# Modulation steps of the second norm, regrouped between the stages of MLA's chain

## The reference

```python
def adaln(cond, w, b):
    return jnp.split(jax.nn.silu(cond) @ w + b, 6, axis=-1)   # sh1, sc1, g1, sh2, sc2, g2

def latent_layer(x, mod, cache, rows, cols, p):
    sh1, sc1, g1, sh2, sc2, g2 = mod
    h = rms_norm(x, p['norm1']) * (1 + sc1) + sh1
    (na_q, na_k, na_v), pool_in, mla_q, ckv, kpe, (sq, sk, sv) = project_mixers(h, p)
    ...
    x = x + g1 * (mixed @ p['w_out'])
    return channel_mlp(x, sh2, sc2, g2, p)

mla_q = rms_norm(heads(rms_norm(mla_cq, p['mla_q_a_norm']) @ p['mla_w_uq'], MLA_HEADS), p['mla_q_norm'])
ckv = rms_norm(mla_ckv, p['mla_kv_norm'])
```

## Time and profile before

| | |
|---|---|
| median of 3 runs | 1676.9 us (1673.57 to 1682.08) |
| the profiled execution | 1677.47 us, span 1675.5 us |
| PE busy | 1557.6 us (93% of the span) |
| PE weight loads busy | 1443.7 us (86%) |
| DVE busy | 1119.9 us (67%) |
| ACT busy | 843.8 us (50%) |
| POOL busy | 135.5 us (8%) |
| mean granted clock of TensorE | 0.972 |

### The profile page before, as it was taken

How to read it: one execution, slowest core, us unless ns; L and a number is a source line. 1 busy time by engine, 2 the same in 40 slices (tenths; PEclk the granted TensorE clock), 3 DMA queues, 4 the chain that set the end, 5 groups by cost and what they waited for, 6 DMA issues and landing times.

```text
span 1675.5 us, 29600 instructions
## 1 busy us (share of the span) xinstructions
PE 1557.6 (93%) x11426; PEld 1443.7 (86%) x11426; DVE 1119.9 (67%) x1937; ACT 843.8 (50%) x1477; POOL 135.5 (8%) x99
## 2 busy tenths in 40 slices
PE   6878997899999999999987889978999999999998
PEld 4755895589999999999976569846999999999998
DVE  4554346858788787787565434487677878878763
ACT  3555533767555454454355454357665545445442
POOL 0003003520000000000000130054000000000000
PEclk8999998999999999999999899979999999999999
DMA  9630453302222223222734205441212222322221
GB/s 323 197 115 1 75 148 111 112 26 76 76 76 76 77 76 101 65 88 76 242 111 158 72 1 130 114 151 52 76 51 76 76 77 76 101 72 81 76 76 64
DMA packets 150867, 160.23 MB, mean 96 GB/s; under 512 B 16390, under 2 KB 132808, under 8 KB 150728
## 3 DMA queue, kind: packets, MB, share of 16 engines
q1 hardware_dynamic: 150024, 158.13, 30.7%
q10 hardware_dynamic: 576, 0.16, 0.0%
q0 software_dynamic: 128, 0.05, 0.0%
HBM read 153.41 MB, written 4.65 MB: 94 GB/s over the span
## 4 chain that ended last, share of the span: by engine, by line
PE 76%; DVE 10%; ACT 9%; issue 3%; DMA 2%; ACTq 0%; SPq 0%; DVEq 0%
PE ps L1909 33%; PE ps L2282 20%; PE ps L2046 10%; PE ps L2298 3%; PE ps L1944 2%; PE ps L1888 1%; PE ps L2070 1%; ACT w_hi L905 1%; PE ps L2123 1%; DVE extrema L1561 1%; ACT pt_c L905 1%; PE ps L2101 1%; DVE extrema L1544 1%; PE ps L2018 1%; PE ps L1918 1%
## 5 line engine op out<-in xcount | busy, mean ns | idle before, releaser
L905 ACT ACTIVATE w_hi<-w_raw 128x512 fp32r<-128x512 f32 (+1 forms) x242 | 189.1, 781 | 196.4 <-PE ps L1909 91.1
L2282 PE MATMUL ps<-x_hi,w_hi 128*128 128x322 f32 x784 | 244.3, 312 | 0.6 <-DVE us L1736 0.6
L2282 PE MATMUL ps<-x_hi,w_lo 128*128 128x322 f32 x784 | 243.5, 311 | 0.0
L2282 PE MATMUL ps<-x_lo,w_hi 128*128 128x322 f32 x784 | 243.4, 310 | 0.0
L1909 PE MATMUL ps<-z_hi,w_hi 128*128 128x384 f32 (+1 forms) x1024 | 233.7, 309 | 0.0
L1909 PE MATMUL ps<-z_hi,w_lo 128*128 128x384 f32 (+1 forms) x1024 | 233.1, 309 | 0.0
L1909 PE MATMUL ps<-z_lo,w_hi 128*128 128x384 f32 (+1 forms) x1024 | 233.1, 309 | 0.0
L1331 DVE TENSOR_TENSOR w_lo<-w_raw,w_hi 128x512 fp32r<-128x512 f32 x212 | 146.8, 692 | 36.0 <-ACT w_hi L905 27.7
L1909 PEld LDWEIGHTS ps<-z_hi,w_hi 128*128 128x128 f32 x1024 | 157.2, 188 | 0.0
L1909 PEld LDWEIGHTS ps<-z_lo,w_hi 128*128 128x128 f32 x1024 | 156.2, 188 | 0.0
L1909 PEld LDWEIGHTS ps<-z_hi,w_lo 128*128 128x128 f32 x1024 | 156.2, 188 | 0.0
(11 more groups left out here) (299 smaller groups left out, 2968.4 us busy)
## 6 DMA issues: line engine op xcount, KB each, us to landing
w_raw<-in_mlp_w SPq DMA_DIRECT2D x64, 1024.0 KB, 5.3
ada_own<-in_w_ada SPq DMA_DIRECT2D x54, 512.0 KB, 4.5
w_raw<-in_w_in SPq DMA_DIRECT2D x14, 1024.0 KB, 9.0
ada_mix<-in_w_ada SPq DMA_DIRECT2D x21, 512.0 KB, 7.3
ada_room<-in_w_ada SPq DMA_DIRECT2D x15, 512.0 KB, 9.1
w_raw<-in_w_out SPq DMA_DIRECT2D x8, 768.0 KB, 5.2
ada_first<-in_w_ada SPq DMA_DIRECT2D x6, 512.0 KB, 9.0
x_in<-in_x_sample SPq DMA_DIRECT2D x1, 2048.0 KB, 8.6
```

What stands on the lines that cost most here:

```text
L905: do(nc.scalar.activation(out, in_, ACT.Copy), sem)
L2282: last = M.matmul(bank(b, XW), w[r][:, k, :], x_of(x, x_name)[:, k, :], start=k == 0 and q == 0 and not more, stop=k == 3 and q == 2, skip ...
```

## The change

```diff
@@ -619,7 +619,7 @@
         def late_ticks(l, stage):
-            cuts = (0, 0, 4, 9, 14, 18)
+            cuts = (0, 0, 4, 8, 12, 18)
             return range(cuts[stage], cuts[stage + 1])
```

## The result

The changed kernel takes 1689.31 us (median of 10 runs, 1684.92 to 1695.68) against 1678.75 us (10 runs, 1673.57 to 1683.65) of the kernel before: a ratio of 1.0063 with a 95% interval of 1.0044 to 1.0082, some 10.6 us slower. The profiled execution of after has a span of 1687.6 us, 12.1 more than that of before.

What follows compares the result with a forecast made beforehand. TensorE work was taken to bound four fifths of the chain, but dependent steps MLA's front. Waits of 7.8 us plus 3.4 of lower clock gave 11.2 on 1677.5, 1688.7; the median lies 0.6 lower, so 1688.1, range 1682 to 1697.

Steps and rivals of the forecast that it cites:

- The wait of turn 3 behind the norm of k: Stage 4: turn 3 waits for DVE's reduce of turn 2, queued behind that norm; +4.39 and 3.4 us, 7.8 in all.
- The earlier q transposes: Stage 3: with units 12, 13 and turn 2 gone, they start 1.96 us earlier in layer 0, 2.51 in layer 1.
- Unit 8 out of stage 2 at nothing: Stage 2: no gain, since the wait for DVE's norm of ckv ends the stage, not unit 8.
- The clock over naq: Stage 4: PE's stand of 5.4 us halves the clock for 3.4 us; 1.7 us a layer, 3.4 in all.
- The loads: Unit 12's load goes out at about 99.3 instead of 81.4; were it late, turn 3's wait would hide it.
- Nothing gives it back: After stage 4: later DMAs are issued on waits for PE's progress and move along, so no time returns.
- A: Rival, stage 4: turn 2's reduce does not hold turn 3; not slower, 1675.7 us; chance 0.05.
- C: Rival, stage 4: clock stays low through turn 3, both naq tiles, into transposes; 6.2 us a layer, 1697.1; chance 0.12.
- B: Rival: the wait is there, but naq keeps full clock or attention C gains what it loses; 1684.7 us; chance 0.18.

Runs made afterwards that it cites:

- run 2: Only ticks 12 and 13 (unit 12, turn 2, unit 13) move from stage 3 to 4, against the kernel before: 1.0073, 1690.50 against 1680.73 us.
- run 3: Changed kernel, but DVE reduces turn 2 inside the norm of k, ahead of its reciprocal: 1.0025 to the kernel before, 1683.17 us.
- run 4: Changed kernel, but turn 3 writes bank 4, needing no wait for the reduce of turn 2: 1.0026 to the kernel before, 1683.58 us.
- run 6: Changed kernel with naq's two tiles ahead of turn 3 on PE: 1.0007 to the kernel before, 1681.51 against 1680.06 us.
- run 8: The kernel before, unchanged, profiled a second time; q to k 12.17 / 11.36 us.
- run 7: Changed kernel, unit 8 back in stage 2, units 14 and 15 between naq's tiles, turn 3 between k transposes: 0.9987, again 0.9986, to the kernel before.
- run 5: Changed kernel with 30 extra matmuls on PE in the wait before turn 3: 1.0043 to the kernel before, 1687.88 us.
- run 1: Only unit 8 moves from stage 2 to stage 3, against the kernel before: 1.0035, 1686.37 against 1680.73 us.

## Why the prediction was right

The forecast was 1688.1 us against a median of 1676.9, 11.2 more; measured were 10.6 more, between 7.4 and 13.8 by the interval. That the two lie within 1 us is closer than this measurement can tell, and in part luck; the terms below are the better test. (The PE share of the chain, 76%, is three quarters, not four fifths; nothing hangs on it.) The terms, step by step:

- *The wait of turn 3 behind the norm of k*: right in place, cause and size. The runs show the cause from four sides: it comes with ticks 12 and 13 (run 2), more than half of the loss goes, by the ratios, with the reduce earlier (run 3) or with another bank (run 4), and nearly all of it with naq ahead of the wait (run 6). Turn 3 comes 4.94 us later after the cq transposes in layer 0 (4.39 forecast) and 3.17 in layer 1 (3.06 to 3.83, 3.4 taken), 8.1 us against 7.8. In layer 1 after, the q transposes kept the upper clock, so its lower end held. Against the second profile of before it is 2.97 and 3.91, 6.9 us in all; the forecast's 7.8 lies between.
- *The earlier q transposes*: 1.96 and 2.51 forecast, 1.50 and 2.50 measured on cq to q; against the second profile of before 2.64 and 2.53.
- *Unit 8 out of stage 2 at nothing*: right. The idle before ckv's transposes grew to 3.56 us as forecast, and they start 7.42 us after the first cq transpose in both kernels. Layer 0 of the first pair of profiles seems to say otherwise: the clock of 82 to 84 stood at 0.65 before and at 0.50 after, and the first projection started 0.45 us later, which is most of what the 1.50 us above lack. But the second profile of the kernel before has the same late start (8.61 us, run 8), and so have both layers of runs 2 and 7, which keep unit 8 in stage 2. The 0.45 us are a difference from execution to execution and not a price of the emptied stage.
- *The clock over naq*: 1.7 a layer forecast, 1.66 and 1.71 measured; naq's 48 matmuls take 7.16 and 7.22 us (7 to 8 forecast, 5.83 before). Run 5 and the two layers of run 4 show that this is the clock: 6.2 us at 1.00, 7.8 at 0.78. That the stand of PE makes it fall is not shown. It fell in all four layers that have the stand (the changed kernel and run 2), but without one too, in four of the six layers of runs 3 to 5, and in neither layer of run 6, where naq follows unit 15 at once. So the size of the term held, and its cause stays partly open. The Trainium skill's rule that activity releases a throttled array (TensorE: Matmul & The Clock Gate, "What's actually happening") agrees here, 0.50 in the wait and 1.00 from 118. Against a plain reading of it, the clock in layer 0 of run 5 fell when PE was already in dense matmuls.
- *The loads*: I said that a late load would be hidden by the wait. It was: units 14 and 15 waited 0.58 and 0.88 us, PE's idle before turn 3 shrank from the 5.4 us of the forecast to 3.81, and turn 3 did not move. Runs 1 and 3 show the other side: where the wait is gone, these loads are the next limit. I had weighed a late load for unit 12 and not for 14 and 15.
- *Nothing gives it back*: outside the two stretches from cq to k the spans differ by 0.6 us in all (0.7 less ahead of them, 1.6 more between them, 0.3 less behind).
- Of the rivals, A fails with the wait in both layers. C fails: the clock was back within naq. B fails: naq lost the clock in both layers, and attention C gave nothing back. It was longer, 59.6 / 59.3 us against 57.9 / 57.2, in layer 1 by just more than the 2 us that the prediction had called a sign against it; but the second profile of the kernel before has 60.5 / 59.1, so this is within what that kernel does by itself. In other kernels naq can keep the clock: layer 0 of run 4 did, behind idles of 0.84 and 0.77 us, where layer 1 lost it behind 0.85 and 0.77.

## What to carry to other kernels

When steps are regrouped by hand, count a turn and its drain as one: two turns through one buffer in one group make the second wait for wherever the other engine's drain stands in its order, here behind a whole norm. The price is set by what is queued behind the waiting instruction. Putting the independent tiles ahead of the wait took the loss from 10.6 us to about 1. Moving a consumer later also moves the load that reuses its buffer, and this stays invisible as long as another wait covers it (run 1).

## What the runs showed of the hardware that I had not expected

One stretch of the program, from the start of the first MLP to the first cq transpose of layer 1, takes one of two times in the eleven profiles: 481.1 us in six of them, the changed kernel's among them, and 485.6 to 485.8 in five, whatever the edit. The kernel before shows both. In its two profiles the stretch 845 to 860, in the first norm of layer 1, reads, first the one then the other (where the stretch of 481 us begins, the second is 1 us behind the first):

```profile
845.00:860.00 15.00, 12.32 (x156) 7.84 (x148) 8.87 (x21) 5.69 (x10) 0.00 (x0) 1.00 0.54 167
```

```profile
845.00:860.00 15.00, 13.79 (x121) 9.92 (x123) 6.46 (x16) 3.58 (x6) 0.00 (x0) 0.77 0.46 131
```

The granted clock falls there in one run and not in the other, with PE over 80% busy in both. From the first score of attention C to the pool's first product it took 154.3 to 160.0 us over the same profiles, also with different low stretches. The two profiles of the kernel before differ by 7.3 us in span, and these places hold more than all of it (4.5, 2.5 and 3.4 us; other stretches go the other way). So they probably make up much of the 10 us by which runs of one kernel differ; an edit worth 2 us, as run 7, is barely seen through them by the median and is plainer in the stretch between two fixed points. Why the clock falls at 845 in some runs stays open.
